# Two transformer blocks on one NeuronCore: the first two feed-forward pairs interleaved operand by operand, with a reordered start

## What is computed

```python
def swiglu(x, w_in, w_out):
    gate, up = jnp.split(x @ w_in, 2, axis=-1)
    return (jax.nn.silu(gate) * up) @ w_out

x = x + 0.5 * swiglu(rmsnorm(x, ffn1_norm_g[l]), ffn1_w_in[l], ffn1_w_out[l])
```

## Time and profile before

| | |
|---|---|
| median of three runs | 1939.83 us (1939.72 to 1943.83) |
| profiled execution, own time | 1945.08 us |
| profiled execution, span of the trace | 1943.0 us |
| TensorE busy (matmul) | 1903.3 us, 98% of the span, 8752 instructions |
| VectorE, ScalarE, GpSimd busy | 1032.3, 783.0, 240.5 us |
| mean granted TensorE clock | 0.988 |

### The profile page before, as it was taken

The page is one execution under the profiler, slowest core; times in us unless marked ns, Lnnn a source line. Parts: engine busy times, 40 slices in busy tenths (PEclk is TensorE's granted clock), DMA queues, the critical chain, the costliest instruction groups (busy, mean ns, idle before and its releaser), DMA issues.

```text
span 1943.0 us, 21345 instructions
## 1 busy us (share of the span) xinstructions
PE 1903.3 (98%) x8752; PEld 1571.7 (81%) x8752; DVE 1032.3 (53%) x1297; ACT 783.0 (40%) x1046; POOL 240.5 (12%) x264
## 2 busy tenths in 40 slices
PE   7999999999999999999999999999989999999997
PEld 5788888878888888888888888888877888888885
DVE  6444434347354666564444334655564877774345
ACT  4332322236443555433223222555554444443234
POOL 5000001201300111140000022100003100000212
PEclk9999999999999999999999999999989999999998
DMA  4423232342241222422222332312213232323331
GB/s 146 163 89 106 87 108 88 105 153 92 76 141 60 93 76 82 137 97 98 98 98 97 98 98 97 111 64 68 74 44 103 82 109 87 108 88 109 98 104 59
DMA packets 51074, 188.98 MB, mean 97 GB/s; under 512 B 6345, under 2 KB 6345, under 8 KB 50081
## 3 DMA queue, kind: packets, MB, share of 16 engines
q1 hardware_dynamic: 46224, 166.74, 26.0%
q0 software_dynamic: 4176, 19.83, 3.0%
q10 hardware_dynamic: 576, 1.05, 0.1%
HBM read 179.18 MB, written 11.03 MB: 98 GB/s over the span
## 4 chain that ended last, share of the span: by engine, by line
PE 95%; DVE 3%; ACT 1%; issue 0%; DMA 0%; DVEq 0%; ACTq 0%; POOLq 0%
PE psum L1675 95%; DVE xl L1090 1%; DVE wl L1093 1%; PE psum L2027 0%; DMA cols<-in_cols 0%; ACT at L766 0%; ACT wh L766 0%; DVE x L1087 0%; DVE az L1090 0%; DVE R L1125 0%; DVE at L1446 0%; DVE fta L1087 0%; DVE tm L1331 0%; ACT R L766 0%; DVE xl L1093 0%
## 5 line engine op out<-in xcount | busy, mean ns | idle before, releaser
L1675 PE MATMUL psum<-xh,wh 128*128 128x512 f32 x1760 | 697.1, 396 | 14.8 <-DVE xl L1090 11.6
L1675 PE MATMUL psum<-xl,wh 128*128 128x512 f32 x1760 | 687.7, 391 | 0.0
L1675 PE MATMUL psum<-xh,wl 128*128 128x512 f32 x1760 | 687.5, 391 | 0.0
L1093 DVE TENSOR_TENSOR wl<-wraw,wh 128x1024 fp32r<-128x1024 f32 (+1 forms) x313 | 405.4, 1303 | 388.1 <-ACT wh L766 387.5
L766 ACT ACTIVATE wh<-wraw 128x1024 fp32r<-128x1024 f32 (+1 forms) x313 | 325.7, 1050 | 382.1 <-PE psum L1675 380.1
L1675 PEld LDWEIGHTS psum<-xh,wh 128*128 128x128 f32 x1760 | 332.1, 189 | 94.5 <-issue 22.6
L1675 PEld LDWEIGHTS psum<-xl,wh 128*128 128x128 f32 x1760 | 332.1, 189 | 70.1 <-issue 2.9
L1675 PEld LDWEIGHTS psum<-xh,wl 128*128 128x128 f32 x1760 | 331.9, 189 | 70.1
L1539 POOL TENSOR_TENSOR ssq<-x 128x512 f32<-128x512 f32 x6 | 6.2, 1039 | 717.3 <-DVE x L1173 454.0
L1675 PE MATMUL psum<-wh,xh 128*128 128x512 f32 (+1 forms) x256 | 88.2, 344 | 0.4 <-ACT zv L766 0.4
L1675 PE MATMUL psum<-wh,xl 128*128 128x512 f32 (+1 forms) x256 | 86.0, 336 | 0.0
(11 more groups left out here) (299 smaller groups left out, 2245.7 us busy)
## 6 DMA issues: line engine op xcount, KB each, us to landing
wraw<-in_w_ffn SPq DMA_DIRECT2D x87, 512.0 KB, 3.3
wraw<-in_w_down SPq DMA_DIRECT2D x44, 512.0 KB, 3.3
wraw<-in_w_up SPq DMA_DIRECT2D x44, 512.0 KB, 3.5
wraw<-in_w_qg SPq DMA_DIRECT2D x28, 512.0 KB, 3.3
wraw<-in_w_att SPq DMA_DIRECT2D x24, 512.0 KB, 3.3
wraw<-in_w_dn SPq DMA_DIRECT2D x22, 512.0 KB, 3.3
wraw<-in_w_zu SPq DMA_DIRECT2D x16, 512.0 KB, 3.3
wraw<-in_w_zv SPq DMA_DIRECT2D x8, 512.0 KB, 3.4
```

The lines of the kernel that those rows point to most:

```text
L1093: return e.tensor_tensor(dst, src, hi.bitcast(F32), ALU.subtract)
L1675: return e.matmul(dst, lhsT, rhs, start=start, stop=stop, skip_group_check=skip)
```

## The change

All of it lies in the first stage of the program.

1. **Order of pairs.** Pairs 0 and 1 are taken together: for each x tile, six matmuls of pair 0 and then six of pair 1. Units 1 and 2 swap places, so that units 0 and 1 serve x tiles 0 to 3 (pairs 0 and 1) and units 2 and 3 serve tiles 4 to 7. Units 0 and 1 are each loaded and split in two parts, of 256 and 768 columns.
2. **Loads.** SyncE issues, in this order: x tile 0, the first parts of units 0 and 1, x tile 1, the second parts, x tiles 2 and 3, unit 2, x tiles 4 to 7. Each x tile has a semaphore of its own. The eight gain columns of this norm come by a load that ScalarE issues first; GpSimd loads the rest of `cols`.
3. **Squares.** ScalarE squares the x tiles (four ahead of unit 3's split, four behind unit 4's) and GpSimd only adds them, once all eight `xl` are there.
4. **Nine matmuls** of ones by ones into bank 7 stand ahead of all others on TensorE; nobody reads them. GpSimd prepares the ones first.
5. The sum over `ssq` is taken one unit later (unit 4, contraction tile 1), and the small product `gfa` moves behind the last `xl` on VectorE.

```diff
@@ make_plan, ffn
+        if f == "a":
+            split(2)
+            for half in range(2):
+                if half:
+                    split(3)
+                    split(4)
+                for kk in range(4):
+                    for p in range(2):
+                        step("pair", f, p, 2 * half + p, half, kk)
+                    step("sq", gen, 4 * half + kk)
+            split(5)
+            waiting = [0, 1]
+        for p in range(2 if f == "a" else 0, 22):
...
     for j in range(8):
-        if j in (0, 2):
-            step("split0", j // 2)
+        if j < 2:
+            step("split0", j)
+        elif j == 2:
+            step("split0", 2)
+            step("split0", 3)
         step("xs", "g1", j)
-        if j == 3:
-            split(1)
-        step("sq", "g1", j)
-    ffn("a", "g1", "gmix", 0, 2, {(3, 2): (0,), (3, 3): (1, 2)},
+    step("gfa")
+    ffn("a", "g1", "gmix", 0, 2, {(4, 1): (0,), (4, 2): (1, 2)},
...
+    units[1], units[2] = units[2], units[1]
+    PARTS = ((0, slice(0, 256)), (1, slice(0, 256)), (0, slice(256, 1024)), (1, slice(256, 1024)))
@@ SyncE
+                e.dma_start(x[:, 0, :], D["xT"][:, 0, :]).then_inc(s_x[0], 16)
+                for i, (u, r) in enumerate(PARTS):
+                    e.dma_start(wraw[:, u, r], units[u][:, r]).then_inc(s_w0[i], 16)
                     if i == 1:
-                        load(1)
-                load(2)
+                        e.dma_start(x[:, 1, :], D["xT"][:, 1, :]).then_inc(s_x[1], 16)
+                for j in range(2, 8):
+                    e.dma_start(x[:, j, :], D["xT"][:, j, :]).then_inc(s_x[j], 16)
+                    if j == 3:
+                        load(2)
@@ ScalarE
+            if kind == "init":
+                e.dma_start(cols[:, 0:8], D["cols"][:, 0:8]).then_inc(s_g1, 16)
...
+            elif kind == "sq" and a[0] == "g1":
+                j = a[1]
+                act(tmpa[:, j - 1, :] if j else ssq[:, :], x[:, j, :], ACT.Square).then_inc(sq1_a.sem, 1)
@@ GpSimd
+                    if j:
+                        e.wait_ge(*xs_lo.at("g1", 7))
+                        e.wait_ge(*sq1_a.at(j))
+                        if j >= 2:
+                            e.wait_ge(*sq.at(g, j - 1))
+                        e.tensor_tensor(ssq[:, :], ssq[:, :], tmpa[:, j - 1, :], ALU.add).then_inc(sq.sem, 1)
@@ TensorE
+            if kind == "init":
+                e.wait_ge(s_const, 2)
+                for i in range(9):
+                    mm(bank(7), onesr[:, :], onesr[:, :].unsqueeze(1).to_broadcast([128, 4, 128]))
```

More of the change, by code:

```diff
@@ L572, in wh_done @@
     def wh_done(u):
-        return s_wh, u + 2
+        return s_wh, u + 3
     def wl_done(u):
-        return s_wl, u + 2
+        return s_wl, u + 3
     s_w = [sem(f"s_w{i}") for i in range(3)]
-    s_wa = sem("s_wa")
-    s_par = sem("s_par")
-    s_x = [sem(f"s_x{i}") for i in range(4)]
+    s_w0 = [sem(f"s_w0{i}") for i in range(2)] + s_w[0:2]
+    s_par, s_g1 = sem("s_par"), sem("s_g1")
+    s_x = [sem(f"s_x{j}") for j in range(8)]
     s_tb = sem("s_tb")
@@ L733, in _ @@
             if kind == "init":
[L734 to L738, removed]
-                    if i == 1:
-                        load(1)
-                load(2)
-            elif (kind == "split" or (kind == "split0" and a[0] == 1)) and (u := a[0] if kind == "split" else 0) + 3 < NU:
+                e.dma_start(x[:, 0, :], D["xT"][:, 0, :]).then_inc(s_x[0], 16)
+                for i, (u, r) in enumerate(PARTS):
+                    e.dma_start(wraw[:, u, r], units[u][:, r]).then_inc(s_w0[i], 16)
+                    if i == 1:
+                        e.dma_start(x[:, 1, :], D["xT"][:, 1, :]).then_inc(s_x[1], 16)
[3 more added lines that the diff above has]
+                        load(2)
+            elif (kind == "split" or (kind == "split0" and a[0] >= 2)) and \
+                    (u := a[0] if kind == "split" else a[0] - 2) + 3 < NU:
                 e.wait_ge(*wl_done(u))
@@ L768, in _ @@
         for kind, *a in plan:
[L769 to L773, removed]
+            if kind == "init":
+                e.dma_start(cols[:, 0:8], D["cols"][:, 0:8]).then_inc(s_g1, 16)
+            elif kind == "split0":
+                u, r = PARTS[a[0]]
+                e.wait_ge(s_w0[a[0]], 16)
+                act(wh[:, u, r], wraw[:, u, r], ACT.Copy).then_inc(s_wh, 1)
+            elif kind == "sq" and a[0] == "g1":
+                j = a[1]
+                act(tmpa[:, j - 1, :] if j else ssq[:, :], x[:, j, :], ACT.Square).then_inc(sq1_a.sem, 1)
             elif kind == "split":
@@ L783, in _ @@
                 if g == "g1":
[L784 to L785 removed]
+                    e.wait_ge(s_g1, 16)
+                    e.wait_ge(s_x[j], 16)
                     scale = col("g1", j)
@@ L1095, in _ @@
         for kind, *a in plan:
-            if kind == "init":
+            if kind == "gfa":
                 e.wait_ge(s_par, 16)
@@ L1099, in _ @@
             elif kind == "split0":
[L1100 to L1103, removed]
+                u, r = PARTS[a[0]]
+                e.wait_ge(s_wh, a[0] + 1)
+                low(wl[:, u, r], wraw[:, u, r], wh[:, u, r]).then_inc(s_wl, 1)
             elif kind == "split":
@@ L1132, in _ @@
                 tmp = TMP[f]
-                e.wait_ge(*unit_done(U0[f] + 2 * p + 1))
+                e.wait_ge(*unit_done(2 + p if f == "a" and p < 2 else U0[f] + 2 * p + 1))
                 if p == 0:
@@ L1517, in _ @@
             if kind == "init":
-                e.dma_start(cols[:, :], D["cols"]).then_inc(s_par, 16)
                 e.memset(ones[:, :], 1.0).then_inc(s_const, 1)
+                e.wait_ge(s_const, 1)
+                e.tensor_copy(onesr[:, :], ones[:, :]).then_inc(s_const, 1)
+                e.dma_start(cols[:, 8:], D["cols"][:, 8:]).then_inc(s_par, 16)
                 e.memset(eps6[:, :], 1e-6).then_inc(s_const, 1)
                 e.memset(eps5[:, :], 1e-5).then_inc(s_const, 1)
-                e.wait_ge(s_const, 1)
-                e.tensor_copy(onesr[:, :], ones[:, :]).then_inc(s_const, 1)
                 e.affine_select(out=ident[:, :], in_=ones[:, :], pattern=[[-1, 128]], compare_op=ALU.is_equal,
```

18 lines of the change are left out of this document (9 added, 9 removed).

## The result

The changed kernel takes 1932.58 us (median of six runs, 1931.40 to 1936.02), the kernel before 1939.78 (six runs, 1936.73 to 1943.83). The ratio is 0.9962 [0.9952 to 0.9971]: 7.2 us faster, at the place and by nearly the amount that was forecast (1932.0).

What follows compares the result with a forecast made beforehand. VectorE's splits were taken to bound the first stage up to 26.3 us. Unit 3 at 20.5 plus 21.5 us puts unit 6 at 42.0 instead of 49.76, 7.8 us less: 1932.0 us, range 1930 to 1936.3.

Steps and rivals of the forecast that it cites:

- The squares: First stage, VectorE: GpSimd's squares slow its subtractions; an xl takes 0.88 us without GpSimd, against 1.57 before.
- Start of real work: TensorE's first real matmul, after x tile 0 and unit 0's first part land: 6.4 us, against 9.68 before.
- the gains in time: ScalarE's separate load of the gain columns: lands between 4.0 and 5.7 us, taken as 4.0; the upper end costs 0.9.
- Unit 3 is late next: Unit 3's copy waits on ScalarE until 18.6 us, its subtraction takes 1.9; TensorE starts it at 20.5 after waiting 1.2.
- From there: TensorE from unit 3 to unit 6: 21.5 us, so unit 6 starts at 42.0 and the 0.41 us wait there goes.
- The sum: TensorE's sum over ssq at 32.7 us: GpSimd's seven adds end by 28.2 to 32.1, so it does not wait.
- Nine matmuls: Ahead on TensorE, 2.0 to 5.9 us, to raise the clock by 6.8: worth 0.8 us at most.
- the arrival of x: Loads of x at the start: same bytes as before in another order, the last tile landing at 13.3 us.
- unit 1's part the tightest: VectorE's split of unit 1's second part: ready at 9.9 us, before TensorE comes to it at 10.6.
- The rival of slow loads: Loads in small pieces stay near 245 GB/s: x tile 7 lands 5.4 us later, time 1937.4; chance 0.09.
- spans behind unit 6 that differ by over 3 us: Sign against the forecast: the part behind unit 6, where the plan is unchanged, differing by over 3 us between kernels.
- slower by the clock: Attention stage: another stage's granted clock falls too, costing 10 us against 7.8 gained, 2 us slower, 1942; chance 0.03.

Runs made afterwards that it cites:

- e2: The changed kernel with the squares back on GpSimd, multiplied and added as each x tile lands, none on ScalarE: 1939.27 us.
- e3: The kernel before with only the squares moved to ScalarE behind the last xh and GpSimd's adds held until the last xl: 1935.55 us.
- e5: The changed kernel with two of the four squares ahead of unit 3's copy on ScalarE moved behind it: 1932.32 us.
- e1: The changed kernel without its nine unread matmuls: 1932.89 us.
- e7: The changed kernel with units 0 and 1 cut into parts of 512 and 512 columns instead of 256 and 768: 1933.53 us, one run.
- e6: The changed kernel with GpSimd's load of the rest of cols moved behind the last xl: 1931.77 us, one run.
- e9: The changed kernel with x in four loads of two tiles instead of eight, the first pair ahead of all weights: 1934.08 us, one run.
- e12: The e5 kernel with the gains loaded from SyncE's queue right behind x tile 0 instead of by ScalarE: 1932.96 us.
- e8: The changed kernel with all of cols loaded by ScalarE at the start and none by GpSimd: 1933.86 us, one run.
- e11: The e10 kernel with this norm's gains loaded by ScalarE and the rest of cols by GpSimd behind the ones: 1933.67 us.
- e4: The kernel before with only the nine unread matmuls added ahead: 1940.17 us.
- e10: The kernel before, old order of pairs and loads, with the nine matmuls, ScalarE squares in two groups of four, and adds after the last xl: 1933.83 us.

## Why the prediction was right, step by step

**Right.** *The squares.* The earlier trace rows carried the argument, and e2 and e3 show both directions: `xl` 1.59 and 0.71 us, unit 6 at 49.13 and 44.45. The rule in "GPSIMD Engine Reference" of the Trainium skill, section Specifications, that GpSimd and VectorE contend when a VectorE instruction has two SBUF inputs, agrees with this too, in the part that spoke against the adds: unit 3's subtraction took 1.98 beside them (1.9 forecast) and 1.23 in the earlier trace rows.
*Start of real work.* 6.22 against 6.4, the gains in time.
*Unit 3 is late next.* Yes, a wait of 1.17 for 1.2, and e5 shows that the squares ahead of its copy cause it. *From there* 21.44 us against 21.5, and no wait at unit 6.
*The sum.* The adds ended at 29.0, in the range of 28.2 to 32.1. They were quicker than the earlier trace rows: 1.29 alone and 2.06 beside VectorE; ScalarE's squares started 0.52 us apart, not 0.63.
*Nine matmuls.* Forecast as worth 0.8 at most; e1 shows no gain from them at unit 6. That the clock held behind them (steps of 0.23 from 6.22) was in part luck: the sum allowed two slow steps, and e5, e2 and e7, whose start differs in nothing or in little, had none, three and eight.

**Off.** The gain at unit 6 was 7.0, not 7.8, and unit 3 came at 21.30, not 20.5. The term that was mis-sized is the arrival of x. I took it from the slices of before, on the ground that the bytes are the same and only their order differs. For unit 2's copy to start at 14.0, x tile 4 had to be there by 11.4, as four copies of 0.65 us lie between; it came at 12.57. Timeline of ScalarE after, the copies that matter (start us, us, instruction, idle before):

```profile
7.53 0.73 ACT L786 ACTIVATE xh<-x,cols 128x512 fp32r<-128x512 f32 x1 [0.33 <-DMA x<-in_xT]
...
12.57 2.69 ACT L786 ACTIVATE xh<-x,cols 128x512 fp32r<-128x512 f32 x4 [1.11 <-DMA x<-in_xT]
15.17 1.04 ACT L786 ACTIVATE wh<-wraw 128x1024 fp32r<-128x1024 f32 x1
```

Forecast for the third row was 14.0: it starts 1.2 us late. Quicker squares gave back 0.4, and unit 3 was 0.8 late. What the runs showed in place of before's slices is a pause of the loads from 4.0 to 6.5 us, at 96 to 250 GB/s, which left 0.47 MB less moved by 10 us: 1.1 us at the 420 GB/s that followed. The same delay stands in the slices: I had unit 1's second part behind 1.73 MB (with `cols`), which the earlier trace rows reach at 7.1 us; after, they are reached at 8.3. Timeline of VectorE after, both second parts:

```profile
9.29 1.87 DVE L1117 TENSOR_TENSOR wl<-wraw,wh 128x768 fp32r<-128x768 f32 x2 [0.25 <-ACT wh L786]
```

The second of them ended at 11.2, not 9.9, and TensorE still came to it later (six matmuls after 10.30). But the first, unit 0's, is needed twelve matmuls after the start and not eighteen, at 9.4, and was ready at 10.3: the wait of 0.94. I had called unit 1's part the tightest and left unit 0's out. This cost nothing, as unit 3's wait hid it. The rival of slow loads was thus right in direction at less than a quarter of its size (1.2 us for 5.4), but not in its mechanism as I wrote it: the rate of the start did not hold for all bytes; it fell further, and from 6.5 to 15 us was 379 or more. Whether small pieces are the reason is not settled by e6 to e9 and e12; only e9, with x in four loads, lost most of the pause.

**Wrong as a test.** I wrote that spans behind unit 6 that differ by over 3 us would speak against the forecast. They differ by 6.3 us, and by 8 among kernels whose code behind unit 6 is the same. I had read the clock's dips in the attention stage from one execution and taken them for fixed. The rival "slower by the clock" lived from the same error. Clock 0.83 and 0.97 after has the same mean as 0.90 and 0.90 before; what differs most is the window at 1200.

## What to carry to other kernels

Before speeding up a start-up stage, ask which engines touch SBUF beside the one that binds: moving 1 us multiplies from GpSimd to a half-idle ScalarE and the adds behind the stage halved VectorE's time for an `xl` and gave three quarters of this gain. New orders came to a microsecond or less, not told from nothing, and warm-up matmuls to nothing that could be told, as a later wait hides them: test each part alone. Where executions differ by as much as the effect, read a fixed point in the trace behind which nothing changed, and let medians of several runs answer for the rest.

## What the runs showed of the hardware

- **Unread matmuls ahead do not fix the clock.** The first real matmuls behind nine identical ones stepped by 0.23 us in five kernels of eleven (after, e5, e6, e8, e11). In e4 and e9 they did, but went back to 0.43 within 1.3 us. In e2 (until 7.4), e7 (10.1), e10 (11.6) and e12 (10.7) they stepped by 0.43 from the first. The nine themselves took 3.70 to 4.07 us in after, e4, e6, e8, e9 and e11, so the clock had risen among them. They took 4.21 us, all at 0.43, in e2, e5, e7, e10 and e12: of these five only e5 went on at 0.23. Among the other six, the two that fell back had the longest pauses behind the nine, 1.97 us (e4) and 2.03 (e9) against 0.92 to 1.64. The pause alone does not set it: one of 1.97 us later in e2 (in front of 11.58) and the one of 1.88 in the earlier trace rows did not lower the clock, one of 2.06 later in e4 did. Nor does the order of the program: after and e5 are the same up to unit 2's split and began at 1.42, and their nine took 3.87 and 4.21 us.
- **The granted clock's column is not enough at the start.** e1's slow steps, the lower level by their 0.43 us, stand in a stretch whose column reads 1.00 (0 to 14 us):

```profile
0.00:14.00 14.00, 7.96 (x28) 6.33 (x28) 6.04 (x9) 7.60 (x11) 1.93 (x10) 1.00 0.85 288
```

- **GpSimd and VectorE slow each other by 1.6 to 2.1 times** with float32 operands of 512 to 1024 columns: `xl` 0.75 and 1.59 us, `wl` 1.23 and 1.98, GpSimd's add 1.29 and 2.06. (The add takes 2.06 when it starts beside a subtraction of a whole unit; beside `xl` it takes 1.6.)
- **The loads at the start paused while the DMA engines were partly idle** (busy 0.3 at the lowest). The lowest slice of 0.5 us between 4.0 and 6.5 us had 84 to 166 GB/s in the eight kernels with x in eight loads and 240 to 332 in the six with four; from 10 to 12 us all moved 381 to 451. e6 to e9 and e12 did not find the mechanism.
